# A two-layer hybrid decoder step: the mixer two units ahead of the page compression, and a 64-token tile in two column halves

## What is computed

```python
h = x @ w_in + b_in                       # mixer: 1024 -> 3 x 2048
a, gl, z = jnp.split(h, 3, axis=-1)
u = a * jax.nn.sigmoid(gl)
up = jnp.concatenate([state, u], axis=1)  # samples; prompts are padded with zeros
y = conv31(up, dw_w) + dw_b               # depthwise, 31 taps
y = jax.nn.silu(layer_norm(y, ln_g, ln_b)) * jax.nn.silu(z)
x1 = layer_norm(ALPHA * x + y @ w_out, ...)
...
# second layer, cached keys and values of the sample sequences:
h = jnp.einsum("sd,sdh->h", pe, w1) + b1  # the compressor's bias
for j in range(2):
    h = h + parts[j][:, j:j + nc]         # parts: chunks of 16 tokens times w1
kc = jnp.einsum("bcgh,hd->bcgd", jax.nn.silu(h), w2)
```

## Time and profile before

| | |
|---|---|
| three timed runs | 1782.03, 1784.23 (median), 1786.17 us |
| the profiled execution | 1785.66 us, span of its instructions 1784.1 us |
| TensorE busy | 1642.5 us, 92% of the span |
| weight loads (beside the matmuls) | 1070.9 us, 60% |
| VectorE busy | 875.2 us, 49% |
| ScalarE, GpSimd busy | 498.4 us (28%), 179.9 us (10%) |
| mean granted TensorE clock | 0.951 of full speed |
| moved by DMA | 160.56 MB, 90 GB/s over the span |

### The profile page before, as it was taken

The page is one execution under the profiler, slowest core; times in us unless marked ns, Lnnn a source line. Parts: engine busy times, 40 slices in busy tenths (PEclk is TensorE's granted clock), DMA queues, the critical chain, the costliest instruction groups (busy, mean ns, idle before and its releaser), DMA issues.

```text
span 1784.1 us, 24182 instructions
## 1 busy us (share of the span) xinstructions
PE 1642.5 (92%) x7065; PEld 1070.9 (60%) x7065; DVE 875.2 (49%) x1940; ACT 498.4 (28%) x1079; POOL 179.9 (10%) x336
## 2 busy tenths in 40 slices
PE   1999749999999999999989999997999979999897
PEld 1766536666666667743433366366778747777753
DVE  0467647888788754211320010016777763454334
ACT  0134223444444422210000000022666632333100
POOL 3012101111111000000000000002000024232100
PEclk6799969999999999999999999988999999999789
DMA  9557645766766526111002256103000045554501
GB/s 157 107 94 128 223 93 86 112 93 90 107 101 88 94 86 230 48 48 47 0 6 59 54 144 136 37 3 99 2 1 2 1 141 176 176 178 143 133 36 42
DMA packets 173096, 160.56 MB, mean 90 GB/s; under 512 B 55350, under 2 KB 150969, under 8 KB 172793
## 3 DMA queue, kind: packets, MB, share of 16 engines
q1 hardware_dynamic: 154742, 119.79, 29.9%
q0 software_dynamic: 16384, 33.64, 9.2%
q10 hardware_dynamic: 1864, 5.90, 0.9%
HBM read 152.41 MB, written 16.38 MB: 95 GB/s over the span
## 4 chain that ended last, share of the span: by engine, by line
PE 86%; SPq 4%; DMA 3%; DVE 2%; issue 2%; ACT 1%; POOLq 0%; POOL 0%; DVEq 0%; ACTq 0%
PE bank L1385 20%; PE bank L1456 11%; PE bank L395 11%; PE bank L1729 5%; PE bank L1664 4%; PE bank L1525 4%; PE bank L1801 4%; PE bank L1537 4%; PE bank L1688 4%; PE bank L1564 3%; PE bank L1428 3%; PE bank L1773 3%; PE bank L1678 2%; SPq L471 2%; DMA arena<-in_cmp_w_dram 2%
## 5 line engine op out<-in xcount | busy, mean ns | idle before, releaser
L1385 PE MATMUL bank<-arena 128*128 128x288 f32 x1536 | 401.1, 411 | 0.0
L1385 PEld LDWEIGHTS bank<-arena 128*128 128x128 f32 x1536 | 285.7, 193 | 69.1
L1065 DVE SCALAR_TENSOR_TENSOR arena<-arena 128x512 f32<-128x512 f32 x464 | 313.8, 743 | 0.0
L1456 PE MATMUL bank<-arena 128*128 128x508 f32 x512 | 238.8, 589 | 0.0
L395 PE MATMUL bank<-arena 128*128 128x512 f32 (+3 forms) x480 | 203.4, 571 | 2.7 <-DVE arena L1140 1.1
L781 ACT COPY arena<-bank 128x512 f32<-128x512 f32 x128 | 74.8, 585 | 297.0 <-PE bank L1428 297.0
L395 PEld LDWEIGHTS bank<-arena 128*128 128x128 f32 (+1 forms) x480 | 80.1, 194 | 125.6 <-issue 119.6
L1456 PEld LDWEIGHTS bank<-arena 128*128 128x128 f32 x512 | 97.3, 190 | 74.2 <-issue 60.8
L706 POOL DMA_DIRECT2D arena<-in_cache_kv_dram x128 | 76.6, 598 | 503.1 <-issue 502.9
L1428 PEld LDWEIGHTS bank<-arena 128*128 128x128 f32 x512 | 64.6, 143 | 91.6 <-issue 57.5
L1428 PE MATMUL bank<-arena 128*128 128x128 f32 x512 | 78.0, 275 | 32.4 <-ACT arena L808 32.4
(11 more groups left out here) (213 smaller groups left out, 1819.1 us busy)
## 6 DMA issues: line engine op xcount, KB each, us to landing
arena<-in_cache_kv_dram POOLq DMA_DIRECT2D x256, 128.0 KB, 4.4
arena<-in_cache_kv_dram SPq DMA_DIRECT2D x256, 128.0 KB, 2.6
arena<-in_conv_w_in_dram SPq DMA_DIRECT2D x48, 512.0 KB, 7.1
arena<-in_nsa_w_in_dram SPq DMA_DIRECT2D x64, 128.0 KB, 2.3
arena<-in_cache_win_dram SPq DMA_DIRECT2D x16, 512.0 KB, 4.9
out_dram<-in_cache_win_dram SPq DMA_DIRECT2D x1, 8064.0 KB
arena<-in_nsa_w_in_dram SPq DMA_DIRECT2D x24, 256.0 KB, 2.6
arena<-in_conv_w_out_dram SPq DMA_DIRECT2D x2, 2048.0 KB, 8.1
```

What stands on the lines that cost most here:

```text
L1065: taps.append(ch.mark(dve.scalar_tensor_tensor(part, src, w, part, ALU.mult, ALU.add)))
L1385: last = pe.matmul(bank[pair + h][:, 0:HALF], weights[:, k], xT[:, k, h * HALF:(h + 1) * HALF], start=k == 0, stop=k == KT - 1)
L1456: last = pe.matmul(h, wc[:, s, j, q], x4[:, :, j:j + NC], start=(q == 0 and j == 0), stop=(q == STEPS - 1 and j == 1))
```

## The change

There are four edits.

- **Order.** `LEAD` is 2: the chunk units begin at unit 2 instead of unit 1. There are 18 units rather than 17; units 16 and 17 carry gates 0 to 3, and the column sums stand directly behind the last chunk unit.
- **Small loads.** `s_small` is split: `s_aux` counts seven loads (parameters), `s_w2` three (second compressor weights). TensorE waits for `s_aux` after the first four steps of unit 0, and for `s_w2` ahead of its first use. The state rows and the two halves of the compressor's weights get semaphores and places of their own in the queue.
- **Bias.** GpSimd multiplies the compressor's weights by the position terms and folds 16 rows into one; TensorE sums it over partitions with a single one-column matmul each, at step 5 of units 2 and 3; ScalarE adds `b1`. GpSimd now loads all pages of chunk 0, and its masks come last.
- **Tile of 64.** Each of its matmuls becomes two with 256 moving columns. The second writes partitions 64 to 127 of the bank; both have the same stationary operand. VectorE and ScalarE read the halves in two operations.

```diff
-UNITS_A = CT + 1
+LEAD = 2
+UNITS_A = CT + LEAD
...
+        def side(t, s):
+
+            return bank[t][s * 64:(s + 1) * 64, s * 256:(s + 1) * 256]
...
-                ins = pe.matmul(bank[t][0:r, 0:width], lhs(k, t), slot, start=first, stop=last_k)
+                if t == TT - 1 and width == 512:
+                    for s in range(2):
+                        ins = pe.matmul(side(t, s), lhs(k, t), slot[:, s * 256:(s + 1) * 256], start=first, stop=last_k)
+                else:
+                    ins = pe.matmul(bank[t][0:r, 0:width], lhs(k, t), slot, start=first, stop=last_k)
...
+            load_state(0)
+            load_mixer(1)
+            load_compressor(0)
+            load_state(1)
...
+            def bias_terms(s):
+
+                w = cbw[:, s]
+                pool.wait_ge(wc_in[s], 16)
+                pool.wait_ge(s_aev, 3)
+                ch.link(pool.tensor_tensor(
+                    w, wc[:, s].rearrange("p j q h -> p (j q) h"),
+                    auxT[:, s * 16:(s + 1) * 16].rearrange("p (n o) -> p n o", o=1).broadcast_to([P, 16, P]), ALU.mult))
+                for n in (8, 4, 2):
+                    ch.link(pool.tensor_tensor(w[:, 0:n], w[:, 0:n], w[:, n:2 * n], ALU.add))
+                pool.tensor_tensor(w[:, 0], w[:, 0], w[:, 1], ALU.add).then_inc(cb_sum, 1)
...
-            pe.wait_ge(s_small, 160)
+            def turn_parameters():
+                pe.wait_ge(s_aux, 112)
...
             for u in range(UNITS_A):
-                if u == 1:
-                    pe.wait_ge(s_wc, 32)
-                    pe.wait_ge(s_aev, 3)
-                    for s in range(2):
-                        for n in range(16):
-                            last = pe.matmul(bank[MB][:, s:s + 1], wc[:, s, n // 8, n % 8], auxT[:, s * 16 + n:s * 16 + n + 1],
-                                             start=n == 0, stop=n == 15)
-                    last.then_inc(s_cbp, 1)
                 for q in range(STEPS):
-                    if u:
-                        turn_chunk(u - 1, q)
+                    if u == 0 and q == 4:
+                        turn_parameters()
+                    if u >= LEAD:
+                        turn_chunk(u - LEAD, q)
...
+                    if q == 5 and LEAD <= u < LEAD + 2:
+                        s = u - LEAD
+                        pe.wait_ge(cb_sum, s + 1)
+                        pe.matmul(bank[MB][:, 254 + s:255 + s], cbw[:, s, 0], ones[:, 0:1], start=True, stop=True).then_inc(cb_ps, 1)
...
-            for zi in range(2, CT):
...
+            for zi in range(2 * LEAD, CT):
                 for q in range(4):
                     gate_part(zi, q)
```

More of the change, by code:

```diff
@@ L64, in ring_order @@
         for q in range(STEPS):
-            if u:
-                order["chunk", u - 1, q] = len(order)
-            if q == 5 and u:
+            if u >= LEAD:
+                order["chunk", u - LEAD, q] = len(order)
+            if q == 5 and 1 <= u <= CT:
                 order["tail", u - 1] = len(order)
@@ L240, in build_program @@
         s_aev = sem("s_aev")
[L241 to L242 removed]
+        cb_ps = sem("cb_ps")
         s_pg = sem("s_pg")
@@ L437, in residual @@
             half = xr[0:n, t, nh * 512:(nh + 1) * 512]
-            dve.scalar_tensor_tensor(half, half, ALPHA, product[0:n, :], ALU.mult, ALU.add).then_inc(o_free, 1)
+            if t == TT - 1:
+                for s in range(2):
+                    part = half[:, s * 256:(s + 1) * 256]
+                    last = dve.scalar_tensor_tensor(part, part, ALPHA, product[s * 64:(s + 1) * 64, s * 256:(s + 1) * 256], ALU.mult, ALU.add)
+                last.then_inc(o_free, 1)
+            else:
+                dve.scalar_tensor_tensor(half, half, ALPHA, product[0:n, :], ALU.mult, ALU.add).then_inc(o_free, 1)
             dve.wait_ge(o_free, freed)
@@ L576, in _ @@
             load_permuted(0, used + 24)
-            load_compressor()
+            for s in range(2):
+                load_compressor(s)
             sp.wait_ge(kv_out, 64)
@@ L918, in _ @@
                     act.wait_ge(zz_ev, it * 5 + (t + 4 + (t == 0)))
-                    act.activation(sig[0:n, t % 2], bank[t][0:n, :], ACT.Sigmoid).then_inc(zz_sg, 1)
+                    if t < TT - 1:
+                        act.activation(sig[0:n, t % 2], bank[t][0:n, :], ACT.Sigmoid).then_inc(zz_sg, 1)
+                    else:
+                        for s in range(2):
+                            last = act.activation(sig[s * 64:(s + 1) * 64, t % 2, s * 256:(s + 1) * 256], side(t, s), ACT.Sigmoid)
+                        last.then_inc(zz_sg, 1)
             for t in range(TT):
@@ L1132, in _ @@
                         dve.wait_ge(ring_used, it * RING + (CT + RING))
-                    dve.tensor_copy(kvr[0:n, t, bass.ds(it * 512, 512)], bank[t][0:n, :]).then_inc(kv_ev, 1)
+                    if t < TT - 1:
+                        dve.tensor_copy(kvr[0:n, t, bass.ds(it * 512, 512)], bank[t][0:n, :]).then_inc(kv_ev, 1)
+                    else:
+                        for s in range(2):
+                            last = dve.tensor_copy(kvr[0:n, t, bass.ds(it * 512 + s * 256, 256)], side(t, s))
+                        last.then_inc(kv_ev, 1)
             with dve.Fori(0, 2) as it:
@@ L1524, in _ @@
                     r = ROWS[t]
-                    last = pe.matmul(bank[t][0:r, :], y[:, c, t * P:t * P + r], wo[:, c], start=c == 0,
-                                     stop=c == CT - 1)
+                    if t == TT - 1:
+                        for s in range(2):
+                            last = pe.matmul(side(t, s), y[:, c, t * P:t * P + r], wo[:, c, s * 256:(s + 1) * 256],
+                                             start=c == 0, stop=c == CT - 1)
+                    else:
+                        last = pe.matmul(bank[t][0:r, :], y[:, c, t * P:t * P + r], wo[:, c], start=c == 0,
+                                         stop=c == CT - 1)
                     if t == TT - 1:
@@ L1536, in _ @@
                 for c in range(CT):
-                    last = pe.matmul(bank[t][0:r, :], y[:, c, t * P:t * P + r], wx[:, c], start=c == 0, stop=c == CT - 1)
+                    if t == TT - 1:
+                        for s in range(2):
+                            last = pe.matmul(side(t, s), y[:, c, t * P:t * P + r], wx[:, c, s * 256:(s + 1) * 256],
+                                             start=c == 0, stop=c == CT - 1)
+                    else:
+                        last = pe.matmul(bank[t][0:r, :], y[:, c, t * P:t * P + r], wx[:, c], start=c == 0, stop=c == CT - 1)
                 last.then_inc(o_ps, 1)
@@ L1600, in _ @@
             pe.wait_ge(rlp_in, 128)
-            pe.wait_ge(s_wc, 64)
+            for s in range(2):
+                pe.wait_ge(wc_in[s], 32)
             for n in range(4):
@@ L1800, in _ @@
                     for m in range(8):
-                        last = pe.matmul(bank[n % 8][0:r, :], oT[:, m, t * P:t * P + r], w_o[:, m, nh * 512:(nh + 1) * 512],
-                                         start=m == 0, stop=m == 7)
+                        if t == TT - 1:
+                            for s in range(2):
+                                lo = nh * 512 + s * 256
+                                last = pe.matmul(side(n % 8, s), oT[:, m, t * P:t * P + r], w_o[:, m, lo:lo + 256],
+                                                 start=m == 0, stop=m == 7)
+                        else:
+                            last = pe.matmul(bank[n % 8][0:r, :], oT[:, m, t * P:t * P + r], w_o[:, m, nh * 512:(nh + 1) * 512],
+                                             start=m == 0, stop=m == 7)
                     last.then_inc(o2_ps, 1)
```

181 lines of the change are left out of this document (95 added, 86 removed).

## The result

The changed kernel takes **1755.29 us** (median of four runs, 1753.04 to 1758.95) against 1785.2 us for the kernel before on the same chip (1782.03 to 1788.03): a ratio of 0.9829, 95% interval 0.9803 to 0.9855, so 30.5 us (25.9 to 35.2), or 1.7%, less. It is faster by more than the noise, and the time lies 6 us above the forecast of 1749. But the parts of the sum are not the forecast ones: the column halves give more, and what the rest gives cannot be told from nothing.

The account below looks back on a forecast made before the run. TensorE, busy 92% of the span, was taken to bound the kernel: 1785.66 - 21.4 (start) + 10.2 (hand-over) - 25.8 (halves) + 0.6 (VectorE, ScalarE) = 1749 us. The sum's own range was 1740 to 1757 us, the wider range 1734 to 1777.

Parts of the forecast that it names:

- The halves: 64-token tile's 88 matmul places: two column halves partly overlap on the array, gaining 25.8 us (bounds 0 and 37.8).
- rivals 1 and 3: 64-token tile: 1, halves run in series, 1775 us, chance 0.18; 3, changing halves costs time, no overlap, 1793 us, chance 0.07.
- low 0 runs beside high 1: 64-token tile: in-order starts overlap only half 0's low part with half 1's high part, gaining 0.215 us at 56 places.
- rival 2: 64-token tile: all pairs of column halves run side by side, gaining 37.8 us, 1737 us in total; chance 0.10.
- The 0.6 us for VectorE and ScalarE: End of each output product: reading the 64-token tile in two operations costs 0.3 us each, 0.6 us lost.
- The start: Units 0 and 1, before the first page step: filled wait and unit 1 done early gain 21.4 us (bounds 17.4 and 27).
- a sign of being wrong: Parameter transposes at the start: the prediction is wrong if the parameters still end the first wait at 47 us.
- the forecast times: Start: unit 0's weights land at about 16 us, parameters come at about 43.5 us, first page step near 72 us.
- the bias was put at 0: Compressor bias: GpSimd's two sums, 6 us each, lie hidden behind a page unit and cost TensorE nothing.
- rival 4: Start: GpSimd's earlier page loads or VectorE's convolution hold it back, gain 10 rather than 21.4 us, 1760 us; chance 0.10.
- The copy's wait: TensorE's second wait, 32.35 us, behind the sync engine's 8 MB copy: stays, price 0, bounds plus or minus 4 us.
- The hand-over: Page compression to gate 4: new weight wait of 6.8 us plus 3.4 us from lower clock, 10.2 us lost.

## Why the prediction was right, and where its steps were wrong

**The halves (forecast 25.8 us): mechanism right, size too small.** The two halves do overlap, rivals 1 and 3 fall. The step that failed is "low 0 runs beside high 1", from instructions that start in order: 0.215 us for each of 56 places between 128-row tiles. All pairs run side by side, rival 2: 37.2 us by the lines, 35 us (31 to 39) in the run with the halves alone. Where pairs follow directly, 0.43 us a place was forecast, and 0.42 is there. The 0.6 us for VectorE and ScalarE are not visible as a term of their own.

**The start (forecast 21.4 us): too large.** At the first page step 1.1 us is gained, and unit 1's 15.6: 16.7. Two steps failed. The parameters did not come at 43.5 us, but still ended a wait, at 48.99 us; the prediction had named that, at 47 us, as a sign of being wrong. The reason is GpSimd's page loads, now ahead of the masks, which run beside the transfers that the start needs: the 37 packets of the parameter rows take as long as before (27.5 against 28 us), but begin at 19.8 us instead of 15.7. The run that holds the page loads back has the forecast times; with the rows in two transfers the parameters are in time (39.48 us) although the page loads stay. And **the bias was put at 0**, on the ground that its sums are hidden behind a page unit. They are, for TensorE's own order; but they hold up VectorE, and unit 2 waits 6.6 us for VectorE. They were also too cheap: 9.2 and 10.1 us, where 6 were taken and 8.8 was the upper bound. This is near rival 4: its page loads are what delays the start, and VectorE does hold back unit 2, but because of the sums and not, as it says, because two units pass in 16 us each. Its own price, 11.4 us lost at the start, is near what is seen: the second layer starts 5.2 us later than before with gates 2 and 3 done, so 15.6 - 5.2 = 10.4 us are left of 21.4. Even the forecast first page step would have helped little, as the run with held-back pages shows: behind it VectorE was next.

**The copy's wait (forecast 0): right,** 32.42 against 32.35 us, and for the reason given.

**The hand-over (forecast 10.2 us lost): nearly right.** The wait is 4.4 us instead of 6.8. The lower clock was forecast as a consequence of that wait; it falls before it, and 3.4 of its 10.2 us are there without the wait too. From 10.4 us gained at the second layer 2.2 are left at the output product: 8.2 us lost. Loading gate 4 sooner gives 5.6 of these back.

**The sum.** One term was missing. Up to the output product the two profiled executions differ by 2.2 us; behind it the changed one is 30.4 us shorter (984.8 against 1015.2), 6.8 less than the halves' 37.2. Instructions of the same shapes and number, those of 288 columns left out (whose 4.7 us lie in the start and the hand-over), were 6.5 us longer in all, 5.5 of it behind the output product. The granted clock goes with it: between the start of the output product and TensorE's last instruction it stood at its lower level for 99 us, 85 in the kernel before, although the mean over the whole execution is the same (0.953, 0.951 before). By estimate, half of these 14 us, up to 7, could be lost by it. Why the clock was low for longer there was not settled. Start and hand-over, 11.2 us by the forecast, came to 2.2, and in the run without the halves to nothing that can be told; the halves came to 37.2 instead of 25.8. The forecast was 6 us from the result because these errors offset each other.

## What to carry to other kernels

When an edit is costed at nothing because it is off the critical path, look at what it holds up on other engines, which transfers it now runs beside, and which engine is late next: here a sum of 10 us on GpSimd cost TensorE a wait of 6.6 us by way of VectorE. Gains ahead of a wait are only worth what the next wait leaves of them, so take the waits in a stage together: of what single edits gained at the start, 4 to 12 us at the first page step, the next waits took half or more, while the largest gain, 31 us by the medians, came from cutting up the 8 MB copy, which the change had left alone. Where a tile fills half of the array's columns, cut the moving side in two halves and alternate them in the program; measure the parts apart, as a total can be right with wrong terms.

## What the hardware showed that was not expected

- Two column halves in 32 bits run fully side by side, starts 6 ns apart and a pair every 0.215 us, also between tiles of 128 rows; and an instruction can start ahead of three earlier ones of the other half.
- While GpSimd added and multiplied in SBUF, VectorE got through one multiply-add on 128 x 512 numbers for each GpSimd operation, however long that one was (4.41 us beside 3.62, 1.21 beside 1.06); without it they follow every 0.67 us.
- A transfer of 31 rows of 8 KB moved one packet after the other; as 16 and 15 rows, the 37 packets of this size took 13 us instead of 27.5.
